# Compressed attention in two batches instead of eight, with the query products and the compression matmuls put in another order around it

## The reference, cut to what matters

```python
def compress(x_raw, pos, w1, w2):
    blocks = x_raw[:, idx] + pos[:, None, :]          # 31 blocks of 32 tokens
    blocks = ...reshape(B, n_cmp, NSA_GROUPS, CMP_BLOCK * HEAD_DIM)
    return jax.nn.gelu(blocks @ w1) @ w2

kc = compress(k_cmp, ...); vc = compress(v_cmp, ...)
s = jnp.einsum('btgjd,bngd->btgjn', q, kc) * scale    # 16 heads x 512 x 31
p_cmp = jnp.where(c_valid, jax.nn.softmax(jnp.where(c_valid, s, NEG_INF)), 0.0)
o_cmp = jnp.einsum('btgjn,bngd->btgjd', p_cmp, vc)
```

## Time and profile before

| | |
|---|---|
| three runs, us | 2203.15, 2197.55, 2194.5 (median 2197.55) |
| profiled execution, us | 2197.66 |
| its span, us | 2195.9 |
| mean granted clock of TensorE | 0.964 |
| PE busy | 2074.9 us, 94% |
| DVE, ACT, POOL busy | 48%, 37%, 13% |

### The profile page before, as it was taken

One profiled execution on the slowest core, in us unless ns is written; L12 is line 12 of the kernel. 1 busy time (PEld: TensorE's weight loads), 2 busy tenths in 40 slices (PEclk: granted clock), 3 DMA queues, 4 the chain that ended last, 5 costly groups with the idle time before them and its releaser, 6 DMA issues.

```text
span 2195.9 us, 25916 instructions
## 1 busy us (share of the span) xinstructions
PE 2074.9 (94%) x10292; PEld 1745.5 (79%) x10292; DVE 1051.0 (48%) x1668; ACT 822.4 (37%) x1526; POOL 283.8 (13%) x271
## 2 busy tenths in 40 slices
PE   7999999999999999999998889788989999999998
PEld 6878888888888888888887778567777888888886
DVE  5437475555344222335546764655655445222333
ACT  5225353334334222334325742255555433222232
POOL 1001000000000000000013431066665000000000
PEclk9997799999999999999998998799999999999999
DMA  5330133333323333332541062111113532333331
GB/s 193 111 91 1 58 112 100 97 96 96 96 68 115 96 96 97 98 99 81 149 129 31 1 215 63 59 43 44 44 44 118 160 92 96 96 96 98 99 100 68
DMA packets 59752, 200.14 MB, mean 91 GB/s; under 512 B 8081, under 2 KB 8113, under 8 KB 59505
## 3 DMA queue, kind: packets, MB, share of 16 engines
q1 hardware_dynamic: 53936, 178.29, 26.4%
q0 software_dynamic: 5696, 20.21, 2.7%
HBM read 181.16 MB, written 8.39 MB: 86 GB/s over the span
## 4 chain that ended last, share of the span: by engine, by line
PE 76%; DVE 8%; ACT 5%; POOL 4%; issue 2%; DMA 2%; DVEq 2%; POOLq 0%; SPq 0%; ACTq 0%
PE ps L649 24%; PE ps L651 23%; PE ps L650 23%; POOL PU L605 4%; DMA raw<-in_w_all 2%; DVE Wl L1658 1%; PE ps L979 1%; PE ps L1064 1%; DVE XN L1698 1%; ACT Pb L1357 1%; DVE HTl L1707 1%; DVEq L2181 1%; ACT XN L1224 1%; DVE AUl L2186 1%; PE ps L824 1%
## 5 line engine op out<-in xcount | busy, mean ns | idle before, releaser
L1658 DVE TENSOR_TENSOR Wl<-raw,Wh 128x1024 fp32r<-128x1024 f32 x307 | 377.9, 1235 | 787.3 <-ACT Wh L1191 786.5
L649 PE MATMUL ps<-HTh,Wh 128*128 128x512 f32 (+1 forms) x1696 | 644.3, 380 | 21.8 <-DVE HTl L1707 10.8
L650 PE MATMUL ps<-HTl,Wh 128*128 128x512 f32 (+1 forms) x1696 | 637.9, 376 | 0.0
L651 PE MATMUL ps<-HTh,Wl 128*128 128x512 f32 (+1 forms) x1696 | 637.9, 376 | 0.0
L1191 ACT CAST Wh<-raw 128x1024 fp32r<-128x1024 f32 x307 | 321.5, 1052 | 820.6 <-DMA raw<-in_w_all 820.5
L649 PEld LDWEIGHTS ps<-HTh,Wh 128*128 128x128 f32 x1696 | 322.6, 190 | 80.0 <-issue 20.8
L651 PEld LDWEIGHTS ps<-HTh,Wl 128*128 128x128 f32 x1696 | 321.6, 190 | 58.2
L650 PEld LDWEIGHTS ps<-HTl,Wh 128*128 128x128 f32 x1696 | 322.4, 190 | 55.7
L649 PE MATMUL ps<-Wh,Yh 128*128 128x512 f32 x528 | 206.1, 390 | 4.3 <-DVE Yl L1834 4.3
L651 PE MATMUL ps<-Wh,Yl 128*128 128x512 f32 x528 | 205.5, 389 | 0.0
L650 PE MATMUL ps<-Wl,Yh 128*128 128x512 f32 x528 | 205.4, 389 | 0.0
(11 more groups left out here) (272 smaller groups left out, 2562.9 us busy)
## 6 DMA issues: line engine op xcount, KB each, us to landing
raw<-in_w_all SPq DMA_DIRECT2D x307, 512.0 KB, 3.6
swp_d<-qkd SPq DMA_DIRECT2D x64, 64.0 KB, 2.8
g_dram<-gst SPq DMA_DIRECT2D x16, 256.0 KB, 4.0
ring<-g_dram POOLq DMA_DIRECT2D x16, 256.0 KB, 3.5
gpre<-in_g_pre POOLq DMA_DIRECT2D x5, 512.0 KB, 5.3
X<-in_x SPq DMA_DIRECT2D x4, 512.0 KB, 5.4
swp_r<-qkr SPq DMA_DIRECT2D x16, 128.0 KB, 3.8
cw1k<-in_cw POOLq DMA_DIRECT2D x1, 2048.0 KB, 10.7
```

Source lines behind the costliest of these rows:

```text
L649: tensor.matmul(dst, a_hi, b_hi, start=start, stop=False)
L650: tensor.matmul(dst, a_hi, b_lo, start=False, stop=False)
L651: return tensor.matmul(dst, a_lo, b_hi, start=False, stop=stop)
L1658: vector.tensor_tensor(Wl[:, s, :], raw[:, s, :], Wh[:, s, :], ALU.subtract).then_inc(w_lo, 1)
```

## The change

Batches of one group over all four query tiles take the place of batches of one group and one tile: 2 batches of 32 x 31 scores for each query row, not 8 of 8 x 31. PE issues as many matmuls and transposes as before. The scores live in two tiles `CS[0]` and `CS[1]`, weighed in place (no `CP`), and the transposes use banks 2, 3 and 4. The parts are also placed differently:

- PE: `rope_q(1)` before `cmp_hidden(0)`; `cmp_scores(0)` right behind `rope_q(3)`; `cmp_hidden(1)` behind it; `cmp_vals` behind `rope_q(4)`; `cmp_turn(0)` before `rope_q(7)`. In `nsa`: `cmp_scores(1)`, then unit scores and gate halves, and `cmp_turn(1)` before the last half.
- ACT: the copy to `ksh` moves behind `query(0)`; `cmp_hidden(1)`'s Gelu stands behind `cmp_exp(0)`, so the function changes to and fro.
- DVE: the second key rotation moves behind two splits of `nst`; `ksl` moves into the query loop; `cmp_weigh(0)`, `spread_hidden` and the clearing of `vcz` stand at query 4.
- POOL: the key blocks of `cA` are built before the load of `cw1v`, the value blocks behind it. `cw1` lies in memory in the order in which it is read (one contiguous run for each partition).

```diff
-    ("cmpa", 0, [0] * 8, [0, 0, 0, 8, 4, 4, 0, 0]),
+    ("cmpa", 0, [0] * 8, [0, 0, 1, 2, 3, 2, 0, 0]),
...
-        CS = at("CS", 64, [P, 2, 8, 32])
-        CP = at("CP", 66, [P, 2, 8, 32])
+        CS = [at("CS0", 36, [P, 32, 32]), at("CS1", 52, [P, 32, 32])]
...
-                load(cw1v[:], t["cw1"][1].rearrange("(j p) n -> p j n", p=P), in_cwv)
-                pl.wait_ge(in_pos, 16)
-                for kv in range(2):
+                def inputs(kv):
...
+                pl.wait_ge(in_pos, 16)
+                inputs(0)
+                pl.wait_ge(yd_out, 16 * TT)
+                load(cw1v[:].rearrange("p j n -> p (j n)"), t["cw1"][1], in_cwv)
+                inputs(1)
...
                 rope_q(0)
+                rope_q(1)
                 cmp_hidden(0)
-                rope_q(1)
-                cmp_hidden(1)
                 rope_q(2)
                 cmp_keys()
                 rope_q(3)
-                cmp_vals()
-                rope_q(4)
                 pe.wait_ge(free[7], FREED["rope_q"][7] + 2)
                 cmp_scores(0)
+                cmp_hidden(1)
+                rope_q(4)
+                cmp_vals()
                 rope_q(5)
+                rope_q(6)
                 cmp_turn(0)
-                cmp_scores(1)
-                rope_q(6)
-                cmp_turn(1)
-                cmp_scores(2)
                 rope_q(7)
-                cmp_turn(2)
-                cmp_scores(3)
...
                 pe.wait_ge(free[7], FREED["rope_q"][7] + 4)
-                cmp_scores(4)
+                cmp_scores(1)
+                unit_scores(0)
                 gate_half(0)
-                cmp_turn(3)
-                cmp_scores(5)
+                unit_scores(1)
                 gate_half(1)
-                cmp_turn(4)
-                cmp_scores(6)
                 gate_half(2)
-                cmp_turn(5)
-                cmp_scores(7)
+                cmp_turn(1)
                 gate_half(3)
-                cmp_turn(6)
-                unit_scores(0)
-                cmp_turn(7)
-                unit_scores(1)
...
+                    if c == 3:
+                        cmp_exp(0)
+                        hidden(1)
...
-                cmp_exp(3)
-                cmp_high(2)
...
+                cmp_exp(1)
+                unit_exps(0)
                 split(CHUNK0["nsa"] + LEAD)
...
                 split(CHUNK0["nsa"] + 1 + LEAD)
...
-                unit_exps(0)
                 unit_exps(1)
+                cmp_high(1)
...
+                keys_out(0)
+                split(CHUNK0["nst"] + LEAD)
+                split(CHUNK0["nst"] + 1 + LEAD)
+                keys_out(1)
                 vector.drain().then_inc(ks_f, 1)
...
+                    if c == 3:
+                        cmp_shift(0)
+                    if c == 4:
+                        cmp_weigh(0)
                         spread_hidden()
...
+                cmp_shift(1)
+                unit_max(0)
+                turn_query(7)
+                unit_gate(0)
+                cmp_weigh(1)
+                gate_out(0)
                 split(CHUNK0["nsa"] + LEAD)
+                unit_max(1)
                 split(CHUNK0["nsa"] + 1 + LEAD)
-                cmp_shift(7)
-                cmp_low(6)
-                cmp_weigh(7)
+                cmp_low(1)
                 gate_out(1)
```

More of the change, by code:

```diff
@@ L1087, in unit_values @@
                         if h % 8 == 0:
[L1088 removed]
+                            for n in range(2):
+                                pe.wait_ge(free[2 + g + n], FREED["cmpa"][2 + g + n] + TURN_USE[g][n] + 1)
                         tensor.matmul(ps[b][:], vcz[:, g, a, :], CAh[:, g, f, :], start=True, stop=False)
@@ L2068, in _, with keys_out @@
                 ve.wait_ge(in_rope, 64)
-                for kind in range(2):
+                def keys_out(kind):
                     turned(SWAP0["nsf"] + kind, swp_n)
@@ L2077, in _ @@
                     last.then_inc(roped, 1)
+                keys_out(0)
+                split(CHUNK0["nst"] + LEAD)
+                split(CHUNK0["nst"] + 1 + LEAD)
+                keys_out(1)
                 vector.drain().then_inc(ks_f, 1)
             if on("nst"):
[L2080 to L2084, removed]
+                split(CHUNK0["nst"] + 2 + LEAD)
                 for tt in range(TT):
@@ L2125, in cmp_shift @@
-                    vector.drain()
[L2126 to L2133, removed]
+                    vector.tensor_tensor(c[:, :, 0:N_CMP], c[:, :, 0:N_CMP], wide(cst[:, g, 0, :]), ALU.subtract).then_inc(cm_s, 1)
@@ L2140, in cmp_weigh @@
[L2140 to L2148, removed]
-                                         ALU.subtract).then_inc(free[3], 1)
+                    vector.tensor_tensor(s_, s_, wide(cst[:, g, 2, :]), ALU.mult).then_inc(cm_p, 1)
@@ L2151, in _, with cmp_low @@
+                def cmp_low(g):
+                    for f in range(2):
+                        ve.wait_ge(ca_hi, 2 * g + f + 1)
+                        vector.tensor_tensor(CAl[:, g, f, :], ps[2 + g + f][:], CAh[:, g, f, :], ALU.subtract).then_inc(free[2 + g + f], 1)
                 vector.drain()
@@ L2155, in _ @@
                     split(CHUNK0["rope_q"] + c + LEAD)
-                    if c >= 5:
-                        cmp_shift(c - 5)
-                    if c >= 6:
-                        cmp_low(c - 6)
-                    if c >= 5:
-                        cmp_weigh(c - 5)
                     if c:
                         turn_query(c - 1)
-                    if c == 2:
-                        spread_hidden()
-                cmp_shift(3)
-                cmp_low(2)
-                cmp_weigh(3)
-                turn_query(7)
+                    if c == 1:
+                        ve.wait_ge(ks_hi, 1)
+                        vector.tensor_tensor(ksl[:].rearrange("p a g n -> p (a g n)"), ksw[:].rearrange("p a g n -> p (a g n)"),
+                                             ksh[:].rearrange("p a g n -> p (a g n)"), ALU.subtract)
+                        vector.drain()
+                    if c == 3:
+                        cmp_shift(0)
+                    if c == 4:
+                        cmp_weigh(0)
+                        spread_hidden()
+                    if c == 4:
+                        vector.drain()
+                        vector.memset(vcz[:].bitcast(F32), 0.0)
+                        vector.drain().then_inc(vc_zero, 1)
+                    if c == 6:
+                        ve.wait_ge(vc_hi, 1)
+                        for a in range(4):
+                            q = slice(32 * a, 32 * a + 32)
+                            last = vector.tensor_tensor(vcz[q, :, a, HD:P], ps[1][q, 0:2 * HD].rearrange("p (g d) -> p g d", g=2), vcz[q, :, a, 0:HD],
+                                                        ALU.subtract)
+                        last.then_inc(free[1], 1)
+                        cmp_low(0)
             if on("nsa"):
```

150 lines of the change are left out of this document (66 added, 84 removed).

## The result

The changed kernel took 2187.07 us (median of 16 runs, 2171.56 to 2193.45), beside 2196.28 for the kernel before: 0.9943 of it, with a 95% interval of 0.9922 to 0.9964. The forecast was 2162 with a range of 2152 to 2176. The sign was right; of 36 us there were 9.

A forecast was written before the change was run, and what follows sets the result against it. PE's stretch of 127.8 us held 77.3 us of full-clock work, the rest lost to idling and low clock. Work plus remaining waits, low clock and gaps came to 91.8, so 2197.66 - 36.0 = 2161.7, say 2162 us; range 2152 to 2176.

The forecast's parts named there:

- Rival E: Gain not passed on: the loop starts earlier into a transfer or bank that isn't ready; 2197 us, chance 0.03.
- 91.8: Predicted us for the stretch from the first query product's end to the first unit's transpose, 127.8 before.
- The first wait: PE before `cmp_hidden(0)`, for `vhl`: wait gone with 2 us to spare, clock full.
- POOL's inputs: Key inputs before the `cw1v` load, value inputs behind it: ready 15 us before `cmp_hidden(1)`, cost 0.
- The copies of products 3 and 7: PE waits for each copy before the score groups, no longer covered by another product: 0.9 us each.
- Rival A: Clock falls before the values' compression, after the 0.9 us wait and light matmuls; say 2170 us, chance 0.18.
- `cmp_vals`: New PE wait for `hid4`, behind DVE's split, rotation and weighing: 6.4 us, plus 2.6 us of low clock.
- Rival B: No stall at `cmp_vals`, split and rotation undisturbed and weighing overlapped: 9 us less, 2153 us, chance 0.14.
- The stage of units: Unit scores and gate halves: waits of 0.9 us for `unit_exps(0)`, 1.7 for `gate_out(0)`, 0.5 for the bank.
- Rival C: POOL's multiplies in `weigh(0)` hold up `cmp_weigh(1)` on DVE: +2.4 us, 2164 us, chance 0.10.
- The first unit's transpose: Start at 1402.2 instead of 1438.2; its own length, 2.39 us for 10 at half clock, left at no gain.
- Rival D: PE stays at 1.2 GHz between 1338 and 1402: +39 to +53 us, 2201 to 2215 us, chance 0.03.

The follow-up runs named there:

- e1: Changed kernel with the enlarged `cst` in a free place and a filler of its old size, other tiles at old addresses; 2158.64 us, rerun 2159.79.
- e8: e1 with DVE spreading the values' hidden layer before the split, rotation and weighing of chunk 4; 2149.79 us, 0.9764 of the kernel before.
- e6: Kernel before with the weight slots and the region behind them (`Wl`, `Yh`, `Yl`) moved by 64 bytes; 2236.62 us in one execution.
- e9: e8 with DVE making the second key rotation before the split of chunk 1 of `nst`; 2146.07 us, 0.976 of the kernel before.
- e10: Changed kernel with 128 unused bytes behind `cst`, slots and region 768 bytes from their old addresses; 2157.02 us, 0.9812 of the kernel before.

## Why the prediction was wrong

The step that failed is the one on which all sums rest without being one of them: "Behind 1438.2 the loop and the rest of the program keep their order, so a gain here moves the end one for one", and, unsaid, the same for what lies in front. The order was kept, and the price of each pass was not. No term of the sum, and no rival, stands for what the larger `cst` does: 576 bytes in front of `Wl`, `Yh` and `Yl`, which the passes in front of the stretch, in it and behind it all paid for. Rival E said that the gain might not be passed on, but for a transfer or a bank at the loop's start; no such wait came, and the loss was spread over the program. 28.4 us is its size (e1; 27 by the ratios), and with it put back the forecast of 2162 stands beside 2158.64, 2159.79 and 2157.02.

That 91.8 meets 91.7 is luck in part. The waits and the low clock behind them were put at 13.9 us and came to 12.0 (9.0 of waiting and 3.0 of low clock, by the items below); everything else was put at 77.9 and took 79.7. The two groups of scores alone took 3.6 us each where the price was 3.2. The two errors cancel. The steps one by one:

- *The first wait.* Right: none in the profile of the kernel after, `cmp_hidden(0)` 7.06 at 1.00. The margin was called 2 us and is that thin: in one of e1's two profiles it was missed by 1.8, with 4.8 of low clock behind.
- *POOL's inputs.* Right: the values' inputs were ready in time, `cmp_hidden(1)` waited for nothing.
- *The copies of products 3 and 7.* 0.9 each predicted, 0.69 each measured. Rival A, that the clock falls there before `cmp_hidden(1)`, is wrong in every profile of the new order. It has some truth at the second scores (e8).
- *`cmp_vals`.* Right in place, cause and size: 6.4 of waiting predicted, 5.5 measured, with the split at 2.07 and the rotation's slow steps as they were taken from the earlier trace rows; weighing 3.5 predicted, 3.2 in the chain (from 1375.08 to 1378.23). Low clock behind it, 2.6 predicted: `cmp_vals` 1.7 to its successor for 0.8, and `rope_q(5)` 7.64 for 5.54, together 3.0. Rival B is wrong for this kernel; e8 shows what it would take for it.
- *The stage of units.* Predicted 0.9 for `unit_exps(0)`, 1.7 for `gate_out(0)`, 0.5 for the bank: 0.5, 1.2 and 0.4. Rival C is wrong: `cmp_weigh(1)` wasn't held up. DVE's wide product beside POOL's `weigh(0)` took 1.34 where it takes 1.19 alone, and it was POOL that grew, to 5.64 for four where it took 4.28 before; in e8's profile the same four took 4.57 beside the same product, so what POOL loses is not a fixed price. The lines, DVE and then POOL:

```profile
1412.68 1.18 DVE L2129 TENSOR_REDUCE cst<-CS 128x32 f32<-128x992 f32 x1
...
1414.72 1.34 DVE L2138 TENSOR_TENSOR CS<-CS,cst 128x992 f32<-128x992 f32 x1
1415.98 0.68 DVE L2205 COPY gst<-ps 128x512 f32<-128x512 f32 x1
```
```profile
1412.86 5.64 POOL L609 TENSOR_SCALAR PU<-PU,ugg 128x512 f32<-128x512 f32 x4 [39.10 <-DVE ugg L2186]
```

- *The first unit's transpose.* Left at no gain: it took 1.38 instead of 2.39. With the products back at their old price, what lies behind the stretch is 3.5 us shorter than before (2165.2 - 1411.0 = 754.2 in e1's second profile against 757.7); 1.0 of that is this transpose, the rest I did not follow up.
- *Rival D*, that PE stays at 1.2 GHz, is wrong: mean clock 0.96 in the stretch.

What stays open: how PE's reads of two tiles collide, by which rule 64 bytes cost (e6), and why the same stretch of front work ends between 1309.95 and 1320.67 us in profiles with the old prices (before, e1, e8, e9, e10). The granted clock from 1000 to 1290 us was 0.98 in the earliest of them and 0.95 in e1's second, so a part of it is the clock. Single executions of one kernel differ by up to 22 us, the shorter ones with the higher mean clock (2171.56 at 0.983, 2193.45 at 0.972, both the kernel after). So a decomposition of single profiles, like the one at the top, was tested by medians of several runs.

## What to carry to other kernels

A change has a part that the order of the work doesn't show: every tile that grows moves the tiles allocated behind it. Before pricing anything, compare the addresses of the operands of the costly instructions, and compare a stretch that the change doesn't touch in both profiles; 24 matmuls less in the same 400 us told here in one row that time was lost outside the change. Where PE bounds the kernel, start the tiles that it reads together at the same place modulo 256 bytes (a pad of 128 bytes per partition did it here). And behind a new wait, look at what stands in the queue of the releasing engine that could just as well stand behind: moving a fill and two small copies forward took 5.6 us of waiting away.

## What the runs showed of the hardware that was not expected

Passes of 128x512 with 128x128 weights at full clock take 389 ns as the profile models them (0.2267 us from start to start in a product) when all tiles read together, those of the weight load that runs beside the pass among them, start at the same place modulo 256 bytes, 0 or 128; with a difference of 128 bytes 391 to 397 (0.2310 in a query product, where two passes of three are slow). With some tiles moved by 64 bytes they take 392 to 399 in one execution, one pass whose tiles all lie at 192 among them, so no rule is shown for 64. Over the kernel's 10292 matmuls, 6144 of which are such passes, a difference of 128 bytes came to about 27 us, 1.2%, in two kernels. Other differences and other shapes weren't tried.
